# A diagonal state-space, pooling and convolution layer on one core: a new order around the SSM read-out, with state rows turned to full height

## What is computed

```
mod = silu(cond) @ ada_w + ada_b                    # six modulation rows of 1024, for c and c_ctx
h   = rmsnorm(x) * (1 + sc1) + sh1
z   = h @ w_in                                      # 1280 columns: 512 ssm | 256 pool | 512 conv
A:  y = u*d + Re(C_f scan_f(B_f u)) + Re(C_b scan_b(B_b u))   # 32 groups x 16 channels, 64 complex states
    y = gelu(y);  y = y * sigmoid(y @ w_glu + b_glu)
B:  centred window means (2/4/8/16) minus token, per-group linear, scale
C:  a * sigmoid(g) -> depthwise conv, width 31 -> LayerNorm over channels -> silu
x   = x + g1 * (concat(A, B, C) @ w_out)
x   = x + g2 * ((silu(h2 @ w1) * (h2 @ w3)) @ w2);  rmsnorm
```

## Time and profile before

| | us |
|---|---|
| median of 3 runs | 1479.66 (1479.51 to 1480.89) |
| the profiled execution | 1479.28 |
| its span in the profile | 1477.5 |
| TensorE busy, mean granted clock | 1349.0 (91%), 0.931 |
| VectorE, ScalarE, GpSimd busy | 571.9, 365.8, 385.1 |
| read-out in the trace | 328.7 to 424.6 |
| convolution in the trace | 300.7 to 471.9 |
| output projection starts | 514.1 |

### The profile page before, as it was taken

The page is one execution under the profiler, slowest core; times in us unless marked ns, Lnnn a source line. Parts: engine busy times, 40 slices in busy tenths (PEclk is TensorE's granted clock), DMA queues, the critical chain, the costliest instruction groups (busy, mean ns, idle before and its releaser), DMA issues.

```text
span 1477.5 us, 17898 instructions
## 1 busy us (share of the span) xinstructions
PE 1349.0 (91%) x7174; PEld 1190.1 (81%) x7174; DVE 571.9 (39%) x816; ACT 365.8 (25%) x610; POOL 385.1 (26%) x256
## 2 busy tenths in 40 slices
PE   3657998969996899999999999999999999999995
PEld 2147987868862478799999999999999999999894
DVE  2975479983048433322121212122222212121267
ACT  1254351221032534531211111111111111111116
POOL 0800015640022210043322223231313131313115
PEclk9779999985567899999999999999999999999998
DMA  8742154195345123222110101010101010111043
GB/s 271 253 160 63 47 182 137 57 175 158 91 163 237 57 86 123 82 74 78 29 57 28 57 28 57 28 57 28 57 28 57 28 57 28 48 37 43 0 144 128
DMA packets 100520, 130.02 MB, mean 88 GB/s; under 512 B 6270, under 2 KB 78248, under 8 KB 97784
## 3 DMA queue, kind: packets, MB, share of 16 engines
q1 hardware_dynamic: 99408, 126.88, 27.4%
q0 software_dynamic: 640, 2.36, 0.4%
q10 hardware_dynamic: 424, 0.12, 0.0%
HBM read 105.75 MB, written 23.59 MB: 88 GB/s over the span
## 4 chain that ended last, share of the span: by engine, by line
PE 78%; DVE 7%; issue 4%; POOL 4%; ACT 3%; DMA 2%; SPq 1%; ACTq 0%; DVEq 0%; POOLq 0%
PE banks L732 22%; PE banks L733 22%; PE banks L734 22%; DVE banks L1814 3%; PE banks L979 3%; PE banks L981 2%; PE banks L977 2%; DMA ldt<-in_ssm_log_dt 1%; PE banks L819 1%; PE banks L1014 1%; DVE acc L1939 1%; PE banks L1019 1%; ACT sq L1436 1%; SPq L402 1%; POOL psum_w L637 1%
## 5 line engine op out<-in xcount | busy, mean ns | idle before, releaser
L732 PE MATMUL banks<-nt_hi,f13h 128*128 128x384 f32 x1056 | 360.0, 341 | 3.8 <-POOL f13l L690 3.8
L734 PE MATMUL banks<-nt_hi,f13l 128*128 128x384 f32 x1056 | 356.9, 338 | 0.0
L733 PE MATMUL banks<-nt_lo,f13h 128*128 128x384 f32 x1056 | 356.9, 338 | 0.0
L1884 DVE TENSOR_TENSOR fv<-sa,banks 128x384 f32<-128x384 f32 x66 | 36.6, 554 | 486.1 <-PE banks L734 475.1
L732 PEld LDWEIGHTS banks<-nt_hi,f13h 128*128 128x128 f32 x1056 | 199.0, 188 | 5.4 <-issue 5.0
L733 PEld LDWEIGHTS banks<-nt_lo,f13h 128*128 128x128 f32 x1056 | 199.1, 189 | 0.4
L734 PEld LDWEIGHTS banks<-nt_hi,f13l 128*128 128x128 f32 x1056 | 199.2, 189 | 0.0
L696 POOL TENSOR_TENSOR f_lo<-fv,f_hi 128x384 fp32r<-128x384 f32 x66 | 68.2, 1033 | 398.9 <-ACT f_hi L1475 398.9
L732 PE MATMUL banks<-f2h,f_hi 128*128 128x512 f32 x396 | 154.9, 391 | 2.5 <-DVE te L1934 2.4
L733 PE MATMUL banks<-f2l,f_hi 128*128 128x512 f32 x396 | 154.2, 389 | 0.0
L734 PE MATMUL banks<-f2h,f_lo 128*128 128x512 f32 x396 | 154.1, 389 | 0.0
(11 more groups left out here) (275 smaller groups left out, 1772.9 us busy)
## 6 DMA issues: line engine op xcount, KB each, us to landing
fst<-in_ffn_w SPq DMA_DIRECT2D x66, 512.0 KB, 3.7
ad<-in_ada_w SPq DMA_DIRECT2D x20, 1024.0 KB, 8.4
wst<-in_w_in SPq DMA_DIRECT2D x10, 512.0 KB, 5.5
u<-z_dram SPq DMA_DIRECT2D x64, 72.0 KB, 2.6
kbw<-wc_dram SPq DMA_DIRECT2D x8, 576.0 KB, 5.3
wc<-wc_dram SPq DMA_DIRECT2D x16, 288.0 KB, 10.7
x_dram<-xr SPq DMA_DIRECT2D x9, 512.0 KB, 2.9
xe<-x_dram SPq DMA_DIRECT2D x9, 512.0 KB, 4.6
```

Source lines behind the costliest of these rows:

```text
L732: nc.tensor.matmul(out, hi_w, hi_x, start=start, stop=False)
L733: nc.tensor.matmul(out, hi_w, lo_x, start=False, stop=False)
L734: return nc.tensor.matmul(out, lo_w, hi_x, start=False, stop=stop)
L1884: TT(fv[b % 2][:, :], sa[b % 2][:, :], B[2 + b % 2][:, 0:BW], ALU.mult).then_inc(sem("f_made"), 1)
```

## The change

In the projection, each of z blocks 13 to 20 is followed by one `ade_half` and one `kb_half`, and z blocks 21 to 29 run without either; SP loads a w_in tile behind `kbw` instead of ahead of `ade`, and ScalarE's list follows. The pooling matmuls and their evacuations move ahead of the read-out, into other banks. `sst` and `wc` are laid out anew: for each group, partitions 0 to 63 hold the real part and 64 to 127 the imaginary part, and `par` is in the free dimension. The read-out then has three matmuls per group, each over all 128 rows. The copies to `sst` now take 64 partitions each and there are twice as many: GpSimd makes those of e = 0 and 2 (16 copies), ScalarE those of e = 1 and 3 (16), and half of them (where r is not par) go from one half of the partitions to the other. A `j` of the read-out waits for the 8 copies of its own e. `cacc` is split in two, so that the last tap of conv half 0 waits for the pooling matmuls and only that of half 1 for the read-out. The buffers of `ymp`, `lnr` and the w_out tiles move; SP issues the w_out loads at other places and on other semaphores. The waits of ScalarE and VectorE for `y_part_pool` ahead of `y_high(0)` and in `y_low` go.

```diff
-    cacc = at("cacc", [P, 2, VO], O_UZ + 9216)
+    cacc = [at("cacc0", [P, VO], O_WB + 4608), at("cacc1", [P, VO], O_UZ + 9216)]
...
-    ymp = at("ymp", [P, 2, T], O_NT + 18432)
+    ymp = at("ymp", [P, 2, T], O_WS)
...
-    O_OUT = [O_WS, O_WS + 8192, O_ST + 18432, O_ST + 26624, O_BC, O_BC + 8192, O_ST, O_ST + 8192]
+    O_OUT = [O_ST + 18432, O_ST + 26624, O_BC, O_BC + 8192, O_WS, O_WS + 8192, O_ST, O_ST + 8192]
...
-    YB = (3, 5, 6, 7)
+    YB = (5, 6, 3, 7)
...
-            sp.wait_ge(*low_ready(i))
-            w_in_load(i + 2)
+            if i < 5:
+                sp.wait_ge(*low_ready(i))
+                w_in_load(i + 2)
...
+                if n >= 1:
+                    sp.wait_ge(*low_ready(i))
+                    w_in_load(i + 2)
...
-                sp.dma_start(view(wc, (NPAIR * rd + 4 * e) * NC, [[1, 4 * NC]]),
-                             dview(wc_dram, (NPAIR * rd + 4 * e) * NC, [[2 * Q * NC, P], [1, 4 * NC]])).then_inc(sem(f"wc{e}_in"), 16)
+                r, q0 = rd // 2, NPAIR * (rd % 2) + 4 * e
+                sp.dma_start(view(wc, q0 * NC, [[Q * NC, 2], [1, 4 * NC]], NS * r, NS),
+                             dview(wc_dram, (r * Q + q0) * NC, [[2 * Q * NC, NS], [NS * 2 * Q * NC, 2], [1, 4 * NC]])).then_inc(sem(f"wc{e}_in"), 16)
...
-        out_weights(0)
-        out_weights(1)
+            sp.dma_start(wos[n][:, :], dview(A["w_out"], OUT[n] * P * D, [[D, P], [1, D]])).then_inc(sem(WO_IN[n][0]), 16)
...
-                sp.wait_ge(sem("st_copied_act"), 8)
-                sp.wait_ge(sem("st_copied_pool"), 8)
+                sp.wait_ge(sem("st_copied_act"), 16)
+                sp.wait_ge(sem("st_copied_pool"), 16)
...
-            if j == 1:
-                out_weights(2)
-                out_weights(3)
+            if j == 0:
+                out_weights(0)
+                out_weights(1)
...
-        out_weights(4)
-        out_weights(5)
+        out_weights(2)
+        out_weights(3)
+        sp.wait_ge(sem("y_part_pool"), 2)
+        out_weights(4)
+        out_weights(5)
...
-        for e in range(4):
+        for e in (0, 2):
             for r in range(2):
-                q0 = NPAIR + 4 * e
-                nc.gpsimd.tensor_copy(view(sst, (r * Q + q0) * UC, [[UC, 4], [BL, NBL], [1, BL]]),
-                                      view(st, r * Q * SLOTS + q0, [[1, 4], [Q, NBL], [SLOT, BL]])).then_inc(sem("st_copied_pool"), 1)
+                for d in range(2):
+                    q0 = NPAIR * d + 4 * e
+                    for par in range(2):
+                        nc.gpsimd.tensor_copy(view(sst, (par * Q + q0) * UC, [[UC, 4], [BL, NBL], [1, BL]], NS * r, NS),
+                                              view(st, r * Q * SLOTS + q0, [[1, 4], [Q, NBL], [SLOT, BL]], NS * par, NS)).then_inc(sem("st_copied_pool"), 1)
...
-        z_block(13)
-        pe.wait_ge(sem("z_evac"), 10)
-        ade_half(0)
-        z_block(14)
-        ade_half(1)
         pe.wait_ge(sem("bblk"), 2)
         pe.wait_ge(sem("dsel"), 1)
-        for n in range(4):
-            kb_half(n, 0)
-            z_block(15 + 3 * n)
-            if n < 2:
-                ade_half(3 * n + 2)
-            kb_half(n, 1)
-            z_block(16 + 3 * n)
-            if n < 2:
-                ade_half(3 * n + 3)
-            z_block(17 + 3 * n)
-            if n < 2:
-                ade_half(3 * n + 4)
-        for s in range(27, 30):
+        pe.wait_ge(sem("z_evac"), 10)
+        for m in range(8):
+            z_block(13 + m)
+            ade_half(m)
+            kb_half(m // 2, m % 2)
+        for s in range(21, 30):
             z_block(s)
...
-                    for r in range(2):
-                        mm(out, wc[p0:p0 + 64, r, gp, HD:HD + P], sst[p0:p0 + 64, r, gp, :], start=False, stop=False)
-                    for r in range(2):
-                        last = mm(out, wc[p0:p0 + 64, r, NPAIR + gp, 0:P], sst[p0:p0 + 64, r, NPAIR + gp, ::-1], start=False, stop=(r == 1))
...
+        for c in range(8):
+            j = c // 2
+            if c % 2 == 0:
+                pe.wait_ge(sem(f"u{j}_in"), 256)
+                pe.wait_ge(sem(f"wc{j}_in"), 64)
+                pe.wait_ge(sem("st_copied_act" if j % 2 else "st_copied_pool"), 8 * (j // 2 + 1))
+            if c >= 2:
+                pe.wait_ge(sem("y_evac"), 2 * (c - 1))
+            for i in range(2):
+                gp = 2 * c + i
+                for par in range(2):
+                    out = B[YB[2 * (c % 2) + par]][:, UC * i:UC * i + UC]
+                    mm(out, toep[:, 2 * gp + par, :], u9[j % 2][:, (2 * gp + par) % 8, :], start=True, stop=False)
+                    mm(out, wc[:, par, gp, HD:HD + P], sst[:, par, gp, :], start=False, stop=False)
+                    last = mm(out, wc[:, par, NPAIR + gp, 0:P], sst[:, par, NPAIR + gp, ::-1], start=False, stop=True)
+            last.then_inc(sem("y_done"), 1)
+
...
-        for s in range(12, 15):
+        z_out(12)
+        for m in range(8):
+            z_out(13 + m)
+            if m in (1, 4, 7):
+                w_high(6 + m // 3)
+            kb_evac(m // 2, m % 2)
+        for s in range(21, 30):
             z_out(s)
-        w_high(6)
-        for n in range(4):
-            kb_evac(n, 0)
-            z_out(15 + 3 * n)
-            kb_evac(n, 1)
-            z_out(16 + 3 * n)
-            z_out(17 + 3 * n)
-            if n < 3:
-                w_high(7 + n)
-        for s in range(27, 30):
-            z_out(s)
+            if s == 23:
+                w_high(9)
 
...
-                A_(view(sst, (r * Q + 4 * e) * UC, [[UC, 4], [BL, NBL], [1, BL]]),
-                   view(st, r * Q * SLOTS + 4 * e, [[1, 4], [Q, NBL], [SLOT, BL]]), ACT.Copy).then_inc(sem("st_copied_act"), 1)
+                for d in range(2):
+                    q0 = NPAIR * d + 4 * e
+                    for par in range(2):
+                        A_(view(sst, (par * Q + q0) * UC, [[UC, 4], [BL, NBL], [1, BL]], NS * r, NS),
+                           view(st, r * Q * SLOTS + q0, [[1, 4], [Q, NBL], [SLOT, BL]], NS * par, NS), ACT.Copy).then_inc(sem("st_copied_act"), 1)
...
-        state_copy(0)
+        for j in range(2):
+            for b in range(NB):
+                n = NB * j + b
+                act.wait_ge(sem("pool_done"), n + 1)
+                A_(ymp[:, j, b * BW:(b + 1) * BW], B[(3, 7)[n % 2]][:, 0:BW], ACT.Copy, scale=pv[:, V_PS + j:V_PS + j + 1]).then_inc(sem("pool_evac"), 1)
         state_copy(1)
         y_out(0)
         y_out(1)
-        state_copy(2)
...
-                    if j == 0:
-                        dve.wait_ge(sem("y_done"), 8)
-                    STT(cacc[:, j, :], src, w, csum, ALU.mult, ALU.add).then_inc(sem("tap_done"), 1)
+                    dve.wait_ge(*((sem("pool_done"), 6) if j == 0 else (sem("y_done"), 8)))
+                    STT(cacc[j][:, :], src, w, csum, ALU.mult, ALU.add).then_inc(sem("tap_done"), 1)
```

More of the change, by code:

```diff
@@ L489, in _ @@
         sp.wait_ge(sem("pool_done"), 6)
-        sp.wait_ge(sem("ln_scaled"), 2)
+        sp.wait_ge(sem("y_part_dve"), 2)
         sp.wait_ge(sem("y_low_dve"), 4)
@@ L956, in gate_rows @@
             last.then_inc(sem("gate_rows"), 1)
-        pe.wait_ge(sem("toep_in"), 256)
         pe.wait_ge(sem("scan_done"), 1)
-        pe.wait_ge(sem("z_evac"), 30)
         pe.wait_ge(sem("kb_evac"), 8)
[L963 to L971, removed]
-            for i in range(2):
-                gp = 2 * c + i
-                for par in range(2):
-                    out = B[YB[2 * (c % 2) + par]][:, UC * i:UC * i + UC]
-                    p0 = 64 * par
-                    mm(out, toep[:, 2 * gp + par, :], u9[j % 2][:, (2 * gp + par) % 8, :], start=True, stop=False)
-                    for r in range(2):
-                        mm(out, wc[p0:p0 + 64, r, gp, HD:HD + P], sst[p0:p0 + 64, r, gp, :], start=False, stop=False)
-                    for r in range(2):
-                        last = mm(out, wc[p0:p0 + 64, r, NPAIR + gp, 0:P], sst[p0:p0 + 64, r, NPAIR + gp, ::-1], start=False, stop=(r == 1))
-            last.then_inc(sem("y_done"), 1)
-        pe.wait_ge(sem("y_evac"), 16)
         pe.wait_ge(sem("wpool_in"), 64)
@@ L998, in _ @@
                 last.then_inc(sem("pool_done"), 1)
+        pe.wait_ge(sem("toep_in"), 256)
+        pe.wait_ge(sem("z_evac"), 30)
+        pe.wait_ge(sem("pool_evac"), 6)
+        for c in range(8):
[14 more added lines that the diff above has]
+            last.then_inc(sem("y_done"), 1)
+        pe.wait_ge(sem("y_evac"), 16)
         for r in range(2):
@@ L1018, in channel_mean @@
             for j in range(2):
-                last = mm(B[b][:, 0:389], onesm[:, :], src[:, j, 389 * b:389 * b + 389], start=(j == 0), stop=(j == 1))
+                last = mm(B[b][:, 0:389], onesm[:, :], src[j][:, 389 * b:389 * b + 389], start=(j == 0), stop=(j == 1))
             last.then_inc(sem("channels_meant"), 1)
@@ L1351, in _ @@
         y_out(7)
-        for j in range(2):
-            for b in range(NB):
```

(17 more changed lines are left out.)

11 lines of the change are left out of this document (6 added, 5 removed).

## The result

The changed kernel takes 1419.31 us (median of 4 runs, 1414.13 to 1421.83) beside 1479.59 of the kernel before on the same chip: a ratio of 0.958, 95% interval 0.956 to 0.960. It is 60 us faster. The forecast was 1405, so 14 us of the expected gain are missing. The range ended at 1419, and the median lies 0.3 above that end. The profiled execution took 1421.83, with a span of 1420.0.

The account below looks back on a forecast made before the run. It took read-out and conv half 1, one behind the other, as the bound. Run in parallel, the means start at 398.4 instead of 472.02; with 1 us back, 1479.28 - 74.6 = 1404.7, forecast 1405, range 1397 to 1419.

Parts of the forecast that it names:

- Path C: VectorE's conv: starts at 306.7, its 62 taps take 91.6, ends at 398.3 as the later of two paths.
- Path G: Read-out from 327.5, y's trip through DRAM and two GLU tiles: ready for the channel means at 394.7.
- The kbw waits: TensorE in the projection: first kb half waits for kbw until 216.3, then three new waits of 1.8; block 20 6.0 later.
- The copies: State copies on GpSimd and ScalarE: 1.1 each, eight ahead of the read-out taking 8.8, eight more making step 4 wait.
- D: Rival: copies at twice the price, 2.2 each on both engines, time 1419; chance 0.08.
- E: Rival: partition-shifting copies so dear that the kernel is slower, from 5.9 us each; 1513 at 8 us; chance 0.03.
- wc's loads: DMA ahead of the read-out: first four loads take 4 to 8 us, hidden within 12 us of the projection's end.
- The clock: TensorE in the read-out: rises after some 3 us; a step of four groups takes 3.0 warm, 5.9 cold.
- B: Rival: TensorE's clock stays at 1.2 GHz in the read-out, a step takes 5.9, time 1414.5; chance 0.14.
- Row tiles: Old read-out's half-row matmuls: ten passes in 2.99, so nothing overlaps, against the skill's rule that two row tiles run together.
- Full rows give nothing of their own: Rival: with cacc split, the read-out is off the path; called nearly so in the forecast; no chance of its own.
- F: Rival: kbw lands so early that its waits vanish and the conv starts earlier, ending at 392.3; time 1399; chance 0.09.

Follow-up runs that it names:

- kb_pairs: The changed kernel with another projection order (two z blocks, then ade, kb half, ade, kb half, four times; kbw loaded ahead of the second ade): 1401.7 us, ratio 0.946.
- paired_half_height_wc: paired_and_pairs with each of the 16 wc loads filling 64 partitions with two runs instead of 128 with one: 1398.9 us, ratio 0.945.
- half_rows_paired: The changed kernel with the old half-row layout and five matmuls a group, two groups advancing together so neighbours use different row halves and banks: 1418.2 us, ratio 0.957.
- half_rows: The changed kernel with the old half-row layout, copies, wc loads and five matmuls a group; new order and split cacc stay: 1470.9 us, ratio 0.993.
- paired_and_pairs: half_rows_paired in the projection order of kb_pairs, with both u reloads issued ahead of the first yT: 1396.5 us, ratio 0.944.
- old_projection: The changed kernel with the projection's earlier order of z blocks, ade and kb halves and w_in loads: 1418.7 us, ratio 0.958.
- copies_by_direction: The changed kernel with GpSimd making the backward copies and all of e = 2, ScalarE the forward ones of e = 0, 1 and 3: 1421.5 us, ratio 0.960.

## Why the prediction came out as it did

The kernel is faster by what was named: the conv beside the read-out, and full rows at the full clock. The size is off by 17.1 in the profiled execution (1421.83 against 1404.7): the means are 19.4 late (417.8 against 398.4), and 2.3 came back behind them.

- **Path C**: the rate of the taps was right (91.5 against 91.6), the start wrong by 15.1 (321.8 against 306.7), since block 20 ended at 288.9, not 273.8. Conv end 413.3, not 398.3.
- **Path G** was 23.1 later than forecast and took the lead. The projection's end is 13.7 of it (329.0 against 315.3), the copies ahead of the read-out 1.0, read-out to GLU 6.5 (49.9 against 43.4), GLU to means 2.0.
- **The kbw waits** are the step that failed most. The sum implies a first wait of about 3.3 and has three of 1.8, in all 8.7; they were 3.86, 2.66, 3.55 and 2.67, 12.7. And I had not asked what TensorE's clock does behind a wait: three of the four were followed by 5.3 us at 0.53 to 0.56, and behind the third and fourth the low clock ran on into the z block. A kb half took 3.30 at the full clock and 5.37, 5.04 and 5.07 there, the z blocks behind the last two 5.54 and 5.47 instead of 4.41: 7.8 lost. With 4.0 more of waits and 2.2 of a later start upstream (block 13 at 209.9 against 207.7) that is 14.0. The last kb half ended 15.0 late, so 1.0 stays open, and the nine bare blocks took 38.3 instead of 39.6, which leaves the 13.7. That waits and clock cost this much kb_pairs confirms, which takes them away and gains 18.
- **ade's 6.10** went, as forecast. **The pooling matmuls** were hidden.
- **The copies** take 1.15 to 1.22, against 1.1; those that shift partitions take no longer than the others (half of GpSimd's 16 shift, and all 16 lie between 1.146 and 1.199). So D and E fell. Eight on ScalarE ahead of step 4 made the gap forecast as 4 one of 5.49.
- **wc's loads**: I took 4 to 8 us for the first four and called it hidden. They did hide ahead of step 0, but the 16 occupy the DMA engines for twice as long, and the first reload of `u` and y's first trip follow them through the queue. The 6.5 from read-out to GLU can be followed in SP's queue:

```profile
355.19 4.00 SPq L463 DMA_DIRECT2D y_dram<-yb  x8
363.04 0.34 SPq L469 DMA_DIRECT2D yT<-y_dram  x1
363.43 0.91 SPq L451 DMA_DIRECT2D wos<-in_w_out  x2
364.46 4.39 SPq L430 DMA_DIRECT2D u<-z_dram  x8
368.89 4.21 SPq L463 DMA_DIRECT2D y_dram<-yb  x8
376.25 0.34 SPq L469 DMA_DIRECT2D yT<-y_dram  x1
```

  `y_out(3)` ended at 362.56, 20.4 into the read-out and not 18.5: 1.9, of which the clock is 1.0 and the copies 0.9. The next reload was issued 1.9 behind that, because y's first trip landed late (3.85 behind its last issue, where the rows had some 1.7) and two w_out loads follow `yT(0)`. That reload, y and its landing took 2.4 longer than forecast, with the w_out loads just ahead of them in the queue, and the trip of j = 2 took 0.5 longer; -0.2 is left over. So `wc` can stand behind the late first landing, but not behind most of the 6.5. In another order, paired_half_height_wc prices the half rate at 3.1. TensorE's wait of 3.58 ahead of step 6, and the low clock behind it, cost little more, since SP was ready for y's last trip only 0.2 before `y_out(7)` was done. How much of the 2.4 is due to the w_out loads no run shows.
- **The clock** rose 4.9 us into the read-out instead of 3, which is 1.0 of the 6.5; so B fell. The forecast then kept it up to the end, but it fell again behind the waits ahead of steps 4 and 6, and behind the 8.62 ahead of the GLU, whose first tile took 9.40 instead of 8.01. That 1.4 is most of the 2.0 between GLU and means. My reason against B, that the half rows hold the clock down, was half right: half_rows_paired has half rows and a rising clock.
- **Row tiles**: I read in the earlier trace rows that nothing overlaps and wrote that the trace disagrees with the Trainium skill, TensorEngine Tiling (Array Packing), Performance Considerations. The rows were right and the conclusion wrong. In the old list neighbours lie in the same half, so nothing could overlap; put in turn, they do, 3.18 for a pair instead of 5.98. The rule holds for neighbours in different halves, and a list must be ordered so that it has them.
- **Full rows give nothing of their own** once `cacc` is split: refuted, by half_rows they give 51. In the sum C could end last only because full rows make G short. By half_rows_paired what gives the 51 is a read-out that works in all rows at the full clock, by either way.
- **F** (no waits on kbw, 1399) did not occur in the change, but kb_pairs is what it described, and took 1401.7.
- The tail from the means on is 1002.2 instead of 1005.5. The 2.8 by which the means themselves got shorter (3.92 against 6.69) is most of it; I had counted 1.

## What to carry to other kernels

A wait on TensorE can cost clock behind it as well as its length (in 14 of the 16 waits below): price both, and look for an order in which each reload has its own cover. Before data are turned to fill all rows, try the cheaper step of issuing the small matmuls so that neighbours use different rows and banks, which here gave the same time. A layout is also a layout for the DMAs that fill it: what gives the matmul its full height may give the load half, so read the DMA share and the GB/s of the stretch, and not only whether the first transfer was in time.

## What the hardware showed

- Gapless half-row matmuls (K = 64, float32), all neighbours in one half of the rows, kept the granted clock at 0.50 for 95 us. The same matmuls in turn between the halves rose to 1.00 after 3.7 us (4.7 in paired_and_pairs), full-row ones after 4.9 (3.0 in old_projection, 5.9 in copies_by_direction).
- At the full clock, neighbouring half-row passes of 144 columns in different halves take 0.074 each, a full-row pass 0.122.
- In the change, TensorE's waits of 3.86, 3.55 and 2.67 were followed by 5.3 us at 0.53 to 0.56; the one of 2.66 at 239.07 was not (1.00 from 240 on). half_rows, half_rows_paired and copies_by_direction have the same four waits in the projection, 2.19 to 3.93 long, and 11 of these 12 were followed by some 7 us at 0.50 (10 in one case). One of 2.19 was (half_rows, at 237.30), one of 2.19 was not (copies_by_direction, at 259.89), so the length alone doesn't tell them apart; what does, no run here shows.
- Loads on 64 partitions moved 217 to 227 GB/s, on 128 partitions 384 to 407, with packets of 2304 B in both and the DMA engines equally busy (share 1.03 to 1.05). Loads with an outermost dimension of 2 ran at a share of 0.13 and 51 GB/s.
